# Attention core of a diffusion trunk: the softmax guard of both heads as a product and a minimum, and one copy for both heads' transposed probabilities

## The reference, cut to what matters

```python
    m = sink_f
    for s in scores:
        m = jnp.maximum(m, jnp.max(s, axis=-1))
    denom = jnp.exp(sink_f - m)
    for s, vp in zip(scores, values):
        p = jnp.exp(s - m[..., None])
        denom = denom + jnp.sum(p, axis=-1)
        out = out + jnp.einsum('bkgqs,bskd->bqkgd', p.astype(vp.dtype), vp).astype(jnp.float32)
    out = out / jnp.moveaxis(denom, -1, 1)[..., None]
```

## Time and profile before

| what | value |
|---|---|
| median of 3 runs | 2660.65 us (2658.5 to 2661.7) |
| the profiled execution's own time | 2665.53 us |
| its span, first to last instruction | 2663.7 us |
| PE busy | 2573.9 us (97%) |
| PE weight loads | 2383.5 us (89%) |
| DVE busy | 1984.8 us (75%) |
| ACT busy | 1299.1 us (49%) |
| mean granted PE clock | 0.984 of full speed |

### The profile page before, as it was taken

How to read it: one execution, slowest core, us unless ns; L and a number is a source line. 1 busy time by engine, 2 the same in 40 slices (tenths; PEclk the granted TensorE clock), 3 DMA queues, 4 the chain that set the end, 5 groups by cost and what they waited for, 6 DMA issues and landing times.

```text
span 2663.7 us, 43103 instructions
## 1 busy us (share of the span) xinstructions
PE 2573.9 (97%) x15856; PEld 2383.5 (89%) x15856; DVE 1984.8 (75%) x3736; ACT 1299.1 (49%) x2291; POOL 115.5 (4%) x146
## 2 busy tenths in 40 slices
PE   6989999999998999999989999999998999999999
PEld 4966899999998999999879999999997699999998
DVE  3777488888896888888855888888868946754772
ACT  3467365425524663355244662454347936633551
POOL 2000100000012000000101000000100010000000
PEclk9999899999998999999989999999999999999999
DMA  7224122433341334434302335334320012222222
GB/s 292 64 95 148 58 101 104 163 138 118 108 168 48 103 110 160 154 105 146 124 21 72 116 111 184 111 110 153 118 71 29 2 56 72 78 87 64 76 83 78
DMA packets 72274, 279.64 MB, mean 105 GB/s; under 512 B 7888, under 2 KB 11344, under 8 KB 68560
## 3 DMA queue, kind: packets, MB, share of 16 engines
q1 hardware_dynamic: 72144, 277.93, 30.5%
HBM read 274.75 MB, written 3.15 MB: 104 GB/s over the span
## 4 chain that ended last, share of the span: by engine, by line
PE 89%; DVE 7%; issue 2%; ACT 1%; DMA 1%; POOL 0%; SPq 0%; DVEq 0%; ACTq 0%
PE ps L575 20%; PE ps L573 16%; PE ps L574 16%; PE ps L576 15%; PE ps L577 11%; PE ps L792 2%; PE ps L777 2%; PE ps L761 1%; PE ps L634 1%; DVE h L1406 1%; PE ps L687 1%; DVE prob L1609 1%; DVE ada_w L1352 1%; PE ps L828 1%; PE ps L569 1%
## 5 line engine op out<-in xcount | busy, mean ns | idle before, releaser
L575 PE MATMUL ps<-h,w_hi 128*128 128x512 f32 x1768 | 700.5, 396 | 0.0
L573 PE MATMUL ps<-h,w_hi 128*128 128x386 f32 x1768 | 604.8, 342 | 8.2 <-DVE h L1406 4.9
L574 PE MATMUL ps<-h,w_hi 128*128 128x386 f32 x1768 | 602.9, 341 | 0.0
L576 PE MATMUL ps<-h,w_lo 128*128 128x386 f32 x1768 | 598.7, 339 | 0.0
L950 ACT ACTIVATE tail<-ps 128x256 f32<-128x256 f32 x281 | 108.3, 386 | 966.0 <-PE ps L577 965.4
L577 PE MATMUL ps<-h,w_lo 128*128 128x256 f32 x1768 | 503.4, 285 | 0.0
L577 PEld LDWEIGHTS ps<-h,w_lo 128*128 128x128 f32 x1768 | 333.7, 189 | 79.6
L1293 DVE TENSOR_TENSOR w_lo<-w_raw,w_hi 128x1024 fp32r<-128x1024 f32 (+1 forms) x288 | 377.4, 1311 | 4.9 <-ACT w_hi L945 1.7
L573 PEld LDWEIGHTS ps<-h,w_hi 128*128 128x128 f32 x1768 | 339.3, 192 | 11.3 <-DVE h L1406 7.2
L574 PEld LDWEIGHTS ps<-h,w_hi 128*128 128x128 f32 x1768 | 335.8, 190 | 0.0
L575 PEld LDWEIGHTS ps<-h,w_hi 128*128 128x128 f32 x1768 | 334.0, 189 | 0.0
(11 more groups left out here) (166 smaller groups left out, 3890.0 us busy)
## 6 DMA issues: line engine op xcount, KB each, us to landing
w_raw<-in_w_in SPq DMA_DIRECT2D x176, 512.0 KB, 3.6
w_raw<-in_w_out SPq DMA_DIRECT2D x64, 704.0 KB, 4.1
ada_w<-in_ada_t SPq DMA_DIRECT2D x42, 1024.0 KB, 6.3
row_w<-in_ada_t SPq DMA_DIRECT2D x60, 512.0 KB, 3.5
ada_w<-in_ada_w SPq DMA_DIRECT2D x18, 1024.0 KB, 5.0
w_raw<-in_w_qkv SPq DMA_DIRECT2D x24, 512.0 KB, 3.5
w_raw<-in_w_o SPq DMA_DIRECT2D x16, 512.0 KB, 3.5
first_w<-in_ada_w SPq DMA_DIRECT2D x6, 1024.0 KB, 14.3
```

Of the source, the lines that this page charges most:

```text
L573: pe.matmul(main, wh, b[:, 0, 0:MAIN], start=first, stop=False)
L574: pe.matmul(main, wh, b[:, 1, 0:MAIN], start=False, stop=False)
L575: pe.matmul(wide, wh, b[:, :, MAIN:NT], start=first, stop=last, skip_group_check=True)
L576: pe.matmul(main, wl, b[:, 0, 0:MAIN], start=False, stop=last)
```

## The change

The guard of both heads is now made by two operations on two elements a partition: the product of both heads' maxima with the negative scales, and the minimum of that with both negative sinks (every fourth column of `neg_sink`). Before, each head had one operation with two scalar operands, made right behind its reduction. Both reductions now come first. `max_made` counts pieces instead of heads, and both exponentials wait for the piece's guards.

The transposed probabilities of both heads have one tile of `[P, 2, 512]`, and one ACT copy, which waits for both heads' transposes, takes the place of two. `pt_made` counts pieces.

```diff
-            probT = [[sb(f"probT{s}{hd}", [P, 512], F32, a) for hd in range(2)] for s in range(2)]
+            probT = [sb(f"probT{s}", [P, 2, 512], F32, a) for s in range(2)]
...
-                            pe.wait_ge(max_made, 2 * (w - 1))
+                            pe.wait_ge(max_made, w - 1)
...
-                                pe.wait_ge(pt_made, 2 * (w - 1) + hd + 1)
+                                pe.wait_ge(pt_made, w)
...
-                        pe.wait_ge(pt_made, 2 * w + 2)
+                        pe.wait_ge(pt_made, w + 1)
...
-                                               probT[w % 2][hd][:, b * P:(b + 1) * P],
+                                               probT[w % 2][:, hd, b * P:(b + 1) * P],
...
                         act.wait_ge(sink_put, w + 1)
+                        act.wait_ge(max_made, w + 1)
                         for hd in range(2):
                             st = stat[:, w % 2, hd, :]
-                            act.wait_ge(max_made, 2 * w + hd + 1)
...
-                        for hd in range(2):
-                            act.wait_ge(t_done, 2 * w + hd + 1)
-                            act.activation(probT[w % 2][hd][:, b0:b1], ps[:, 4 + hd, b0:b1],
-                                           ACT.Copy).then_inc(pt_made, 1)
+                        act.wait_ge(t_done, 2 * w + 2)
+                        act.activation(probT[w % 2][:, :, b0:b1], ps[:, 4:6, b0:b1], ACT.Copy).then_inc(pt_made, 1)
...
-                            head = 8 * ga + 4 * hd + r
-                            if w - w0 < KT and hd == 0:
-                                dve.wait_ge(q_scaled, KT * a + tile + 1)
-                            dve.tensor_scalar(st[:, 1:2], st[:, 0:1], neg_scale[:, tile, nb, hd:hd + 1],
-                                              neg_sink[:, a, head:head + 1],
-                                              ALU.mult, ALU.min).then_inc(max_made, 1)
+                        st, head = stat[:, w % 2, :, :], 8 * ga + r
+                        if w - w0 < KT:
+                            dve.wait_ge(q_scaled, KT * a + tile + 1)
+                        own.link(dve.tensor_tensor(st[:, :, 1], st[:, :, 0], neg_scale[:, tile, nb, :], ALU.mult))
+                        dve.tensor_tensor(st[:, :, 1], st[:, :, 1], neg_sink[:, a, head:head + 5:4],
+                                          ALU.min).then_inc(max_made, 1)
```

## The result

The changed kernel takes 2670.24 us (median of 9 runs, 2665.37 to 2674.58), the kernel before 2663.12 us (9 runs, 2658.5 to 2667.71): ratio 1.0027, 95% interval 1.0017 to 1.0037. It is 7.1 us slower (interval 4.5 to 9.9). The forecast was 8.4 slower. The profiled execution after took 2674.58 us, with a span of 2672.8.

The account below looks back on a forecast made before the run. PE was taken as the bound, with layer 3's transposes-copy-values loop just under it. Layer 3 +9.1 and layer 0 -0.7 made +8.4 us on 2660.65: 2669.0 us (chance 0.62), own range 2665 to 2672, over the cases 2662 to 2676.

Parts of the forecast that it names:

- The loop closes: Layer 3: transposes, copy, values, next transposes become the limit, 3.44 us per four-block gap and 2.80 per three-block gap.
- Rival (b): Merged copy of about 0.69 us for 1024 columns, so the copy loop never closes; 2657.6 us, chance 0.08.
- The copy's later start, 0.51 and 0.40: Merged copy waits for the second head's transposes, half of L777: 0.51 us later with four blocks, 0.40 with three.
- The sum in layer 3: Layer 3's core: start, seven first gaps, sixteen four-block gaps, eight three-block gaps and context together +9.1 us.
- The guards: DVE in both cores: two new operations of 0.16 us each, 1.73 instead of 1.84, 0.11 less per piece.
- Rival (a): New guard operations as long as the old, 0.27 us each; 2674.5 us, chance 0.15.
- Head 0's lateness: Head 0's guard ready at 1.81 us instead of 1.00 after its reduction began, delaying ACT's exponentials; priced at nothing.
- Context pieces: Last 8 one-block pieces per layer, DVE-paced: 7 x 0.11 us gained; -0.5 in layer 3, -0.8 in layer 0.
- Layer 0: Layer 0's core: start, gaps without a chunk, group changes and context together -0.7 us; gaps with a chunk unchanged.
- The clock: PE's granted clock in layer 3's loop: below 1 between 2030 and 2110 us would prove the forecast wrong.
- Rival (d): Clock falls inside layer 3's loop because PE stands 0.33 in each 3.44 us; 2726 us, chance 0.03.
- Rival (c): Less low clock, as shorter context pieces might hold 2.4 GHz to the end; 2664 us, chance 0.12.

Follow-up runs that it names:

- split_wait: Kernel before with its two copies, the first now also waiting for both heads' transposes: 2673.96 us, ratio 1.0044.
- copy_only: Kernel before with only the copies of both heads merged into one, old guards kept: 2673.80 us, ratio 1.0043.
- copy_reorder: Kernel before with merged copy, old guards, and next transposes and copy put ahead of earlier values and high part: 2658.21 us, ratio 0.9981.
- guard_only: Kernel before with only the new guards (product and minimum), one copy for each head: 2663.08 us, ratio 1.0001.
- guard_reorder: Kernel before with new guards, a copy per head, and next transposes and copy put ahead of earlier values and high part: 2655.63 us, ratio 0.9967.
- after_reorder: Changed kernel with next transposes put ahead of earlier values on PE, and copy ahead of earlier high part on ACT: 2655.79 us, ratio 0.9979 to before.
- before_reorder: Kernel before with only next transposes put ahead of earlier values on PE, and copies ahead of earlier high part on ACT: 2657.98 us, ratio 0.9983.

## Why the prediction was right, step by step

- **The loop closes.** Right, and the cause: shown by split_wait (start alone), copy_only and, from the other side, copy_reorder. Rival (b) is wrong: the copy is 1.025, not under 0.69. The Trainium skill's page "VectorE: DVE Perf Modes", section on the TRN2 errata, says that one large tile pays a fixed latency once and many small ones each time, which speaks for one operation instead of two. It says so of operations that read SBUF, and these copies read PSUM. The 0.06 per piece that the merge saves is real (3.45 against 3.39), and the later start costs seven times that.
- **The copy's later start, 0.51 and 0.40.** The mechanism is right, the size too large. I had halved L777's 1.02 and 0.81. The kernel before has the right number, if its timeline is cut behind the fourth transpose and behind the eighth:

```profile
2088.86 0.65 PE L777 MATMUL ps<-ident,prob 128*128 128x128 f32 x4
...
2088.86 1.09 PE L777 MATMUL ps<-ident,prob 128*128 128x128 f32 x8
```

 Each further transpose adds 0.11, so the second head ends 0.44 behind the first, and with three blocks 0.33. The loops are then 3.00 + 0.44 - 0.07 = 3.37 and 2.46 + 0.33 - 0.06 = 2.73, where 3.38 and 2.73 were measured in all gaps but the long two. The forecast had 3.44 and 2.80: over its 31 gaps that was 1.5 us more than the measured +8.3, and would have been 2.1 more without the long two.
- **The sum in layer 3.** By the timeline's starts, forecast and measured: start -0.2, -0.2; first seven gaps +1.7, +1.1 (17.94 to 18.99); sixteen four-block gaps +5.4, +4.8 (49.60 to 54.42); eight three-block gaps +2.7, +2.4 (19.76 to 22.15); context -0.5, 0.0; together +9.1, +8.2 (with 0.1 in the very first gap, which I had left out). So 1.5 too much in the loops and 0.6 too little in the context and the first gap partly cancelled.
- **The guards.** Right: 162 and 164 ns for 160; first reduction to reciprocal 1.74 (2080.88 to 2082.62) instead of 1.84, forecast 1.73. The Trainium skill's rule to keep down the number of operations, not the semaphores ("VectorE: DVE Perf Modes", "The DRAIN you can't avoid" and the rules for authors), taken as one price for every operation, would have given 1.84: the measurement decides against that reading here, by 0.10 a piece. The new rows, of the changed kernel's timeline:

```profile
2080.88 0.69 DVE L1607 CUSTOM_DVE_ANT_0 prob<-ps,band 128x512 f32<-128x512 f32 x1 [0.36 <-PE ps L764]
...
2082.62 0.16 DVE L1623 RECIPROCAL stat<-stat 128x2 f32<-128x2 f32 x1
```

 Rival (a) is wrong. Head 0's lateness costs nothing in the steady part (guard_only).
- **Context pieces.** Piece to piece it is 1.73 where DVE sets the pace (forecast 1.71), but I had priced seven pieces a layer at 0.11; in layer 3 only three gaps were at 1.82 before, the last gap took 1.90 instead of 1.58, and the last transposes to the projection took 2.70 instead of 2.55. guard_only, without the late copy, gained only 0.1 in layer 3's context: 0.4 in the first five gaps, of which it lost 0.3 in the last two, where half clock had come. So -0.5 became 0.0, and in layer 0 -0.8 became -0.1.
- **Layer 0.** Forecast -0.7, measured -0.2. Ahead of the context the pieces went as forecast but for the four-block ones: three-block gaps without a chunk 2.97 to 2.88, four-block ones +0.01 (forecast +0.07), the two at a change of groups +0.28 and +0.27 (forecast +0.3).
- **The clock.** Rival (d) is wrong: the granted clock stayed full through layer 3's loop, though PE stands in each piece. Rival (c) isn't seen either; half clock lasted longer behind the core. Windows of the changed kernel:

```profile
2030.00:2128.00 98.00, 89.86 (x910) 68.94 (x906) 84.34 (x329) 81.98 (x199) 6.77 (x32) 1.00 0.01 2
...
2142.00:2144.00 2.00, 2.00 (x7) 1.91 (x7) 0.00 (x0) 0.00 (x0) 0.00 (x0) 0.50 0.00 0
2144.00:2146.00 2.00, 2.00 (x12) 1.91 (x12) 0.00 (x0) 0.00 (x0) 0.00 (x0) 0.92 0.00 0
```

 Full clock came back at about 2144.3, 5.9 us behind the first projection (2138.41); in the kernel before it was 3.8 behind it (2131.63):

```profile
2134.00:2136.00 2.00, 2.00 (x9) 1.86 (x9) 0.00 (x0) 0.00 (x0) 0.00 (x0) 0.64 0.00 0
2136.00:2138.00 2.00, 2.00 (x13) 1.91 (x12) 0.00 (x0) 0.00 (x0) 0.00 (x0) 1.00 0.00 0
```

 Two more us at half speed are 1 us of the 2.3 by which the part behind layer 3 was longer. The rest lies at a second stretch at half clock further on: in the changed kernel's trace the granted clock is 0.94 from 2204 to 2206 us, 0.50 to 2208 and 0.70 to 2210, with PE busy throughout, and in the trace of before it is 1.00 from 2190 to 2210. There the changed kernel falls back by 1.5 more (ACT's L998 starts at 2198.36 before and 2206.19 after, 7.8 apart; the operations behind it are 9.3 apart, and 9.1 at the end). guard_only and guard_reorder have such a stretch too, and after_reorder, with the same guards, has none, so no edit is shown to bring it.

So layer 3's sum was 0.9 too high and layer 0's 0.5 too low. In the two traces the cores differ by 8.0, in the medians the kernels by 7.1, for a forecast of 8.4. That the absolute 2669.0 came so close to 2670.24 is partly luck: the change cost 1.3 less than forecast, and the kernel before itself measured 2.5 higher over nine runs than over the three.

## What to carry to other kernels

Before two operations become one, ask what each waited for: the merged one starts when the last producer is done, and where the consumer stands in a loop just under the period, that delay counts, less the loop's slack, however many microseconds the merge takes off the engine's busy time. Write the loop out from the timeline (start, length, hand-over, consumer) and compare it with the period; here the slack was 0.12 us, the later start 0.44 and the shorter copy 0.07, so each four-block gap grew from 3.12 to 3.38. Where such a loop is the limit, put the next piece's producer ahead of this piece's consumer: two exchanged steps in each loop gained 4.5 us on the kernel before (2.4 to 6.9), and the merge, which had cost 11, then cost nothing that can be measured.

## What the runs showed of the hardware

- TensorE's full clock (1.00 granted, 2.4 GHz, instead of 0.50) came 3.2 to 4.0 us after a core's first transposes in some executions, and 4.5 to 6.3 us after them in others. In layer 3 it came early in before, changed, before_reorder and guard_reorder, and late (5.9 to 6.1) in the six others, with no edit that they share. In layer 3 the late rise costs 1.3 us in the first two gaps (7.69 against 6.39). Two profiles that differ by 1 to 3 us in a core's length are to be compared behind these gaps.
- One ACT copy across two PSUM banks has no extra cost for the second bank: 379, 812 and 1025 ns for 256, 768 and 1024 columns lie within 5 ns of the line through the copies of 384 and 512 columns in the earlier trace rows, 0.83 ns a column and about 0.17 us beside them.
